# Unread 256-column products at 73 places of a three-layer transformer kernel's TensorE program

## Chip, cores, metric

One core of a Trainium2 chip runs the whole program in one launch. The metric is the device time of that core in microseconds (us). Lower is better.

## What is computed

The input is `x` of 256 tokens by 1024. Three residual layers follow each other, all in float32: one layer of the first kind, a norm, two layers of the second kind, a norm.

```
first kind:   x += 0.5 * swiglu(rms_norm(x));  x += mixer1(rms_norm(x));  x += 0.5 * swiglu(rms_norm(x))
mixer1:       dilated attention (12 heads) and an RWKV-7 recurrence (16 heads), each gated, summed, @ w_o
second kind:  x += 0.5 * swiglu(rmsnorm(x));   x += mixer2(rmsnorm(x));   x += 0.5 * swiglu(rmsnorm(x))
mixer2:       concat(chunked attention, top-k attention, latent attention) @ w_out
```

The feed-forward part is 1024 to 2816 and back. RWKV-7 keeps a 64x64 state per head and updates it by `S = S diag(w) + (S a) b^T + v k^T`.

## The kernel before

**Tiles.** Tokens lie as two halves of 128. A float32 matrix product is made of three products of rounded parts: each operand is split into a high part (`whi`, `xh`, `yh`) and the rest (`wlo`, `xl`, `yl`), and `mm3` (lines 1418 to 1421) multiplies high by high, high by low and low by high. The small products of attention and of the recurrence are plain float32.

**Weights.** They come in chunks of up to 1 MB into three `raw` buffers by SP's queue. ScalarE writes the high part (`split`, line 1939) and VectorE the low part (`split`, line 2284), in two or four pieces a chunk. A piece stands in those engines' programs between the other work, at the place that the order gives it.

**The order.** The class `Order` writes one list of steps, and every engine runs its share of that list in that order. `do` (line 402) appends a step. Eleven stages follow each other: a feed-forward part (stages 0, 2, 4, 6, 7, 9), mixer1 (stage 1), mixer2 (stages 5 and 8), and norms (stages 3 and 10). In mixer1 the recurrence runs as eight groups of two heads (`group`, steps `r_...`), up to three at a time, woven with dense products by a planner that keeps a clock of estimated times (`PACE`, `woven`). In mixer2 the heads, the top-k index, the latent part and the dense products are generators that take turns.

**PSUM.** There are eight banks in a list of free ones. A step takes the bank at the head, and `give` puts it at the end as soon as the steps that read it are written down. On the chip the first product into a bank waits for the last reader of the tile that was there before (`bank_free`, `freed`).

**Steps that the prediction names.** `r_mean` (line 1771) sums a group's result over its heads. `r_d` and `r_x` (lines 1695, 1702, 1683) are the small products by which a 64x64 triangle is inverted; ahead of each `r_x` GpSimd clears a buffer (line 2886). `turn_merged` (line 1439) transposes mixer1's merged rows, which VectorE writes at line 2489. `proj ... in2 3` is the fourth dense product of mixer2, `latent_up` the one ahead of it. `wout2` and `wo` are the last products of the mixers. `warm` (line 1416) makes 12 and 10 products of a zeroed tile at the very start, which nobody reads.

```
class Slots:
    def take(self, key):
        self.at[key] = self.free.pop(0)
    def give(self, key):
        self.free.append((self.at[key][0], key))
```

Of the kernel before, what the change touches and what calls it, by code (L numbers as in the profile page):

```python
# [10 lines left out]
F32R = mybir.dt.float32r  # L11
# [110 lines left out]
    "proj": (("pe", 0.7),), "proj_out": (("dve", 0.7), ("act", 0.6)),  # L122
}
HOP = 0.25


def const_table():
# [67 lines left out]
class Marks:  # L195


    def __init__(self, nc, ctx):
        self.nc, self.ctx = nc, ctx
        self.sem, self.by, self.n, self.at, self.freer = {}, {}, {}, {}, {}  # L200
        self.real = False
        self.had = {}
# [5 lines left out]
    def begin(self, real):  # L208
        self.real = real
        self.had = {}  # L210
        self.n = dict.fromkeys(self.n, 0)
# [21 lines left out]
    def due(self, eng, *tokens):  # L233

        out = {}
        for t in tokens:
            if not t:
                continue
            name, key = t
            if isinstance(key, int):  # L240
                v = key
            elif self.real:
                v = self.at[name][key]
            else:
                v = self.at[name].get(key, 0)
            if self.had.get((eng, name), 0) < v:
                self.had[eng, name] = v
                out[name] = (self.sem[name], v)
        return list(out.values())


class Dry:
# [44 lines left out]
    def max(self, *a, **k):  # L297
        return self
# [54 lines left out]
class Order:  # L353


    def __init__(self, stages):
        self.stages = stages
        self.chunks = plan(stages)
        self.number = {c[:3]: i for i, c in enumerate(self.chunks)}
        last, self.prev = {}, []  # L360
        for i, c in enumerate(self.chunks):
            self.prev.append(last.get(c[4]))
            last[c[4]] = i
        self.steps = []
        self.bank = Slots(range(8))
        self.slots = {}
        self.n_dma = self.n_split = 0
        self.used = set()
        self.lead_from, self.last_from = (), ()
        self.under_way = []  # L370
        self.now, self.ready = {"pe": 0.0, "act": 0.0, "dve": 0.0}, 0.0
        self.begin()
        for s, st in enumerate(stages):
            if st[0] == "ffn":
                self.ffn(s, st[1])
            elif st[0] == "mix1":
                self.mix1(s)
            elif st[0] == "mix2":
                self.mix2(s, st[1])

    def begin(self):

        self.do("warm", 12)
        for _ in range(3):
            self.feed_dma()
        parts = itertools.chain(self.pieces(4), self.pieces(4))
        for nn in range(2):
            self.do("sumsq", 0, 0, nn)
        self.do("scale", 0, 0)
        for k in (0, 2, 4, 6):  # L390
            self.turn(("x", 0, 0, k), "turn_x", 0, 0, k)
            for _ in range({0: 2, 2: 1, 4: 2, 6: 3}[k]):
                next(parts)
            if k == 4:
                for nn in range(2):
                    self.do("sumsq", 0, 1, nn)
        self.do("warm", 10)
        self.do("scale", 0, 1)
        for _ in parts:
            pass  # L400

    def do(self, *step):
        self.steps.append(step)
        for eng, us in PACE.get(step[0], ()):
            self.now[eng] = max(self.now[eng], self.ready) + us
            self.ready = self.now[eng] + HOP

# [691 lines left out]
def build(nc, stages, x_in, wall, consts, rows, lorap, ebias, out):  # L1099
# [5 lines left out]
    with ExitStack() as ctx:  # L1105
        M = Marks(nc, ctx)
# [5 lines left out]
        def sb(name, shape, dt=F32):  # L1112
            return ctx.enter_context(nc.sbuf_tensor(name, shape, dt))
# [5 lines left out]
        xh, xl = sb("xh", [128, 8, 256], F32R), sb("xl", [128, 8, 256], F32R)  # L1119
        yh, yl = sb("yh", [128, 8, 256], F32R), sb("yl", [128, 8, 256], F32R)  # L1120
        C = sb("C", [128, cbase])
        small = sb("small", [128, 84])

        early = [None] * 6
# [9 lines left out]
        PS = ctx.enter_context(nc.psum_tensor("PS", [128, 8, 512], F32))  # L1134

        def con(name):
            a, w = ctab[name]
            return C[:, a:a + w]

# [226 lines left out]
        def run(eng, table):  # L1366
            for name, *a in P.steps:
                if name == "mark":
                    if eng != "sp":
                        M.mark(eng, ("mark",) + tuple(a))  # L1370
                elif name in table:
                    table[name](*a)

        def sync_program(e):
            due = lambda *t: M.due("sp", *t)

            def rows_in(tt):
                e.dma_start(X[:, tt, :], x_in[tt * 128:(tt + 1) * 128]).then_inc(*M.sig(f"x{tt}", ("x",)))

            def load(i):  # L1380
                w = P.chunks[i][3]
                src = wall[int(offs[i]):int(offs[i + 1])].rearrange("(p w) -> p w", p=128)
                if i == 0:
                    rows_in(0)
                    e.dma_start(C[:, 0:chead], consts[:, 0:chead]).then_inc(*M.sig("ident", ("c",)))
                elif i == 1:
                    rows_in(1)
                elif i == 2:
                    e.dma_start(C[:, chead:cbase], consts[:, chead:cbase]).then_inc(*M.sig("consts", ("c",)))
                if i >= 3:  # L1390
# [16 lines left out]
        def tensor_program(e):  # L1407
            due = lambda *t: M.due("pe", *t)
# [9 lines left out]
            def mm3(o, wa, wb, xa, xb, first, last):  # L1418
                e.matmul(o, wa, xa, start=first, stop=False)  # L1419
                e.matmul(o, wa, xb, start=False, stop=False)  # L1420
                return e.matmul(o, wb, xa, start=False, stop=last)  # L1421

            def turned(tile, w, src, *toks):

                b = bank(tile)
                for t in due(bank_free(tile), IDENT, *toks):
                    e.wait_ge(*t)
                for tt in range(2):
                    i = e.transpose(b[0:w, tt * 128:(tt + 1) * 128], src(tt), ident)
                i.then_inc(*M.sig("pe", (tile,)))  # L1430
# [27 lines left out]
            def gu(s, m, i):  # L1458
                hi, lo = whi[slot_of(i)], wlo[slot_of(i)]
                b = bank(("gu", s, m))  # L1460
                for t in due(bank_free(("gu", s, m))):
                    e.wait_ge(*t)
                for g in range(2):
                    for t in due(half_of(i, g == 0)):
                        e.wait_ge(*t)
                    for k in range(8):
                        c0 = (g * 8 + k) * 128
                        for t in due(*[("dve", ("xl", s, tt, k)) for tt in range(2)]):
                            e.wait_ge(*t)
                        p = mm3(b[:, g * 256:(g + 1) * 256], hi[:, c0:c0 + 128], lo[:, c0:c0 + 128], xh[:, k, :],  # L1470
                                xl[:, k, :], k == 0, k == 7)
                p.then_inc(*M.sig("pe", ("gu", s, m), ("use", i)))
# [438 lines left out]
            def turn_out(s, k):  # L1911
                turn_pair(("ot", s, k), OUT, 8, k, *[("dve", ("o", s, kind, tt)) for kind in ("bc" if k >= 4 else "ab")
                                                    for tt in range(2)])

            run("pe", {"warm": warm, "turn_x": turn_x, "gh_turn": gh_turn, "gu": gu, "down": down, "up": up, "wout": wout, "wo": wo, "wout2": wout2,
                       "proj": proj, "shift_mm": shift_mm, "att_qk": att_qk, "att_score": att_score,
                       "att_turn": att_turn, "att_out": att_out, "turn_ao": turn_ao, "turn_merged": turn_merged,
                       "r_lora": r_lora, "r_norm": r_norm, "r_wide": r_wide, "r_vb": r_vb, "r_ka": r_ka,
# [8 lines left out]
        def scalar_program(e):  # L1927
            due = lambda *t: M.due("act", *t)
            COLS = ("ident", ("c",))
            copy = ACT.Copy  # L1930

            def split(i, q, n, after):
                if q < n:
                    w = P.chunks[i][3]
                    c = slice(w * q // n, w * (q + 1) // n)
                    for t in due((f"raw{i % 3}", ("chunk", i)), P.prev[i] is not None and ("pe", ("use", P.prev[i])),
                                 *(marked(*after) if after else ())):
                        e.wait_ge(*t)
                    e.activation(whi[slot_of(i)][:, c].bitcast(F32R), raw[i % 3][:, c], copy).then_inc(  # L1939
                        *M.sig("whi", ("split", i, q)))  # L1940
# [316 lines left out]
            def turn_out(s, k):  # L2257
                high(xh, k, 8, ("ot", s, k), ("oh", s, k))

            run("act", {"out": out_, "split": split, "sumsq": sumsq, "scale": scale, "turn_x": turn_x, "glu": glu,  # L2260
                        "proj_out": proj_out, "shift_copy": shift_copy, "lora_act": lora_act, "att_qk": att_qk,
                        "att_soft": att_soft, "att_turn": att_turn, "turn_ao": turn_ao, "turn_merged": turn_merged,
                        "r_tanh": r_tanh, "r_exp": r_exp, "r_vb": r_vb, "r_ka": r_ka, "r_dm0": r_dm0,
# [531 lines left out]
        def gpsimd_program(e):  # L2795
# [129 lines left out]
            def gain(s):  # L2925
                row = stages[s][1]
                for t in due(*marked("norm", s - 1)):
# [6 lines left out]
                         "r_var": r_var, "bias8": bias8, "m2_begin": m2_begin, "lat_sq": lat_sq, "gain": gain})  # L2934

        programs = (tensor_program, scalar_program, vector_program, gpsimd_program, sync_program)
        M.begin(False)
        for program in programs:
# [9 lines left out]
        @block.tensor  # L2948
        def _(e):
            tensor_program(e)  # L2950

        @block.scalar
        def _(e):
            scalar_program(e)
# [120 lines left out]
```

## Time and profile before

| | |
|---|---|
| median of 3 runs | 1986.04 us (1985.81 to 1987.86) |
| profiled execution, its own time | 1986.59 us |
| its span, first to last instruction | 1984.8 us |
| TensorE products busy | 1903.7 us, 14176 records |
| VectorE, ScalarE, GpSimd busy | 1116.5, 939.5, 91.2 us |
| mean granted TensorE clock | 0.972 |

A record of a product reaches from its start to its modelled end; products follow each other before the one ahead has ended, so the distance of two starts is what one costs. A float32 product that is not a transposition has two records. The row of the granted clock (PEclk) is in tenths of 2.4 GHz, and 0.50 in a stretch means 1.2 GHz throughout. "Idle before" is the time between the modelled end and the next start.

### The profile page before, as it was taken

What the parts mean: (1) busy time and instruction counts of PE and PEld (TensorE: products, weight loads), DVE (VectorE), ACT (ScalarE), POOL (GpSimd) and SP (SyncE); (2) the same over time, 40 slices, a digit from 0 to 9 for tenths busy, and PEclk for the clock granted to TensorE, in tenths of its full rate; (3) what the DMA queues carried; (4) which work ended last, traced back from release to release, by engine and by line L of the source; (5) the groups of instructions that cost most, each with busy time, mean ns of one, the idle gap of its engine ahead of it and who ended that gap; (6) DMA issues with size and microseconds to landing.
All of it is one profiled execution on the core that took longest, in us unless ns stands there. A gap on an engine that the chain in (4) does not pass through costs nothing.

```text
span 1984.8 us, 33483 instructions
## 1 busy us (share of the span) xinstructions
PE 1903.7 (96%) x14176; PEld 1690.7 (85%) x14176; DVE 1116.5 (56%) x2247; ACT 939.5 (47%) x1827; POOL 91.2 (5%) x187
## 2 busy tenths in 40 slices
PE   9999999999998999999999899999999998989998
PEld 8999878888776799979997686899899987868998
DVE  5565556756444555665555745556455657445554
ACT  5454555423211544544554565445444545655443
POOL 0000001111200000010000000000000000000000
PEclk9999999999878999999999999999999999999999
DMA  6564532221101455625562333456355623333553
GB/s 231 188 233 181 186 134 107 94 84 61 55 27 70 157 178 206 233 86 191 210 229 84 107 115 109 170 186 243 123 172 200 241 94 107 107 144 139 191 181 116
DMA packets 42725, 296.28 MB, mean 149 GB/s; under 512 B 4832, under 2 KB 4960, under 8 KB 10576
## 3 DMA queue, kind: packets, MB, share of 16 engines
q1 hardware_dynamic: 41184, 288.32, 40.8%
q0 software_dynamic: 1392, 5.83, 0.9%
q8 instruction: 111, 1.82, 0.4%
q14 instruction: 38, 0.31, 0.0%
HBM read 293.08 MB, written 1.05 MB: 148 GB/s over the span
## 4 chain that ended last, share of the span: by engine, by line
PE 86%; DVE 8%; ACT 3%; POOL 1%; issue 1%; DMA 1%; POOLq 0%; DVEq 0%; ACTq 0%
PE PS L1419 25%; PE PS L1420 23%; PE PS L1421 23%; DVE wlo L2284 1%; PE PS L1702 1%; PE PS L1683 1%; PE PS L1695 1%; DVE xl L2347 1%; ACT GATE L1950 1%; DVE arena L2424 1%; PE PS L1907 1%; PE PS L1819 1%; PE PS L1599 1%; DVE X L2380 1%; PE PS L1447 1%
## 5 line engine op out<-in xcount | busy, mean ns | idle before, releaser
L2284 DVE TENSOR_TENSOR wlo<-raw,whi 128x512 fp32r<-128x512 f32 (+4 forms) x780 | 616.9, 833 | 211.9 <-ACT whi L1939 206.1
L1939 ACT ACTIVATE whi<-raw 128x512 fp32r<-128x512 f32 (+4 forms) x780 | 534.7, 739 | 148.5 <-PE PS L1421 144.7
L1419 PE MATMUL PS<-xh,whi 128*128 128x256 f32 x1944 | 556.0, 286 | 2.1 <-DVE wlo L2284 2.1
L1421 PE MATMUL PS<-xh,wlo 128*128 128x256 f32 x1944 | 550.8, 283 | 0.0
L1420 PE MATMUL PS<-xl,whi 128*128 128x256 f32 x1944 | 550.7, 283 | 0.0
L1419 PEld LDWEIGHTS PS<-xh,whi 128*128 128x128 f32 x1944 | 373.2, 192 | 8.0 <-issue 2.5
L1420 PEld LDWEIGHTS PS<-xl,whi 128*128 128x128 f32 x1944 | 373.2, 192 | 2.3
L1421 PEld LDWEIGHTS PS<-xh,wlo 128*128 128x128 f32 x1944 | 373.1, 192 | 0.0
L1419 PE MATMUL PS<-whi,yh 128*128 128x512 f32 (+2 forms) x580 | 231.3, 399 | 6.9 <-DVE wlo L2284 5.2
L1420 PE MATMUL PS<-wlo,yh 128*128 128x512 f32 (+2 forms) x580 | 227.9, 393 | 0.0
L1421 PE MATMUL PS<-whi,yl 128*128 128x512 f32 (+2 forms) x580 | 227.0, 391 | 0.0
L1419 PE MATMUL PS<-whi,xh 128*128 128x512 f32 (+4 forms) x480 | 196.2, 409 | 13.6 <-DVE wlo L2284 9.6
L2003 ACT ACTIVATE arena<-PS 128x256 f32<-128x256 f32 x108 | 41.4, 383 | 343.8 <-PE PS L1421 343.8
L1420 PE MATMUL PS<-wlo,xh 128*128 128x512 f32 (+4 forms) x480 | 182.7, 381 | 0.0
L1421 PE MATMUL PS<-whi,xl 128*128 128x512 f32 (+4 forms) x480 | 182.3, 380 | 0.0
L2368 DVE TENSOR_TENSOR arena<-arena,PS 128x256 f32<-128x256 f32 x108 | 45.5, 421 | 231.7 <-ACT arena L2003 231.7
L1419 PEld LDWEIGHTS PS<-whi,yh 128*128 128x128 f32 x580 | 111.3, 192 | 30.5 <-DVE wlo L2284 7.8
L1421 PEld LDWEIGHTS PS<-whi,yl 128*128 128x128 f32 x580 | 111.0, 191 | 23.1
L1420 PEld LDWEIGHTS PS<-wlo,yh 128*128 128x128 f32 x580 | 111.3, 192 | 19.3
L1419 PEld LDWEIGHTS PS<-whi,xh 128*128 128x128 f32 x480 | 92.0, 192 | 40.7 <-issue 13.6
L1421 PEld LDWEIGHTS PS<-whi,xl 128*128 128x128 f32 x480 | 92.2, 192 | 14.9
L1420 PEld LDWEIGHTS PS<-wlo,xh 128*128 128x128 f32 x480 | 92.5, 193 | 11.9
(259 smaller groups left out, 2138.7 us busy)
## 6 DMA issues: line engine op xcount, KB each, us to landing
raw<-wall SPq DMA_DIRECT2D x249, 1024.0 KB, 4.9
raw<-wall SPq DMA_DIRECT2D x12, 768.0 KB, 4.2
raw<-wall SPq DMA_DIRECT2D x8, 968.0 KB, 4.9
raw<-wall SPq DMA_DIRECT2D x4, 896.0 KB, 4.4
arena<-ebias POOLq DMA_DIRECT2D x2, 768.0 KB, 4.8
raw<-wall SPq DMA_DIRECT2D x2, 720.0 KB, 4.1
raw<-wall SPq DMA_DIRECT2D x2, 640.0 KB, 3.9
X<-x SPq DMA_DIRECT2D x2, 512.0 KB, 5.1
```

Source lines behind the costliest of these rows:

```text
L1419: e.matmul(o, wa, xa, start=first, stop=False)
L1420: e.matmul(o, wa, xb, start=False, stop=False)
L1421: return e.matmul(o, wb, xa, start=False, stop=last)
L1447: i = e.transpose(b[:, k * 128:(k + 1) * 128], xn[:, tt, (k0 + k) * 128:(k0 + k + 1) * 128], ident)
L1599: p = e.transpose(b[:, c0 + tt * 128:c0 + tt * 128 + 128], src[:, tt * 128:tt * 128 + 128], ident)
L1683: p = e.matmul(b[ps, u * 32:(u + 1) * 32], W_.T[ps, hh, 0, tt, 0:64], some(W_.Dm[ps, u, :], k, 0), start=True, stop=True)
L1695: p = e.matmul(b[ps, u * 32:(u + 1) * 32], W_.DT[ps, u, :], some(X[ps, u, :], k, 0), start=True, stop=True)
L1702: p = e.matmul(b[ps, u * 32:(u + 1) * 32], X[ps, u, :], some(W_.DT[ps, u, :], k, 1), start=True, stop=True)
L1939: e.activation(whi[slot_of(i)][:, c].bitcast(F32R), raw[i % 3][:, c], copy).then_inc(*M.sig("whi", ("split", i, q)))
L2003: e.activation(g, b[:, 0:256], ACT.Silu).then_inc(*M.sig("act", ("silu", s, m)))
L2284: e.tensor_tensor(wlo[slot_of(i)][:, c], raw[i % 3][:, c], whi[slot_of(i)][:, c].bitcast(F32), ALU.subtract).then_inc(*M.sig("wlo", *[("ha ...
L2368: e.tensor_tensor(g, g, b[:, 256:512], ALU.mult).then_inc(*M.sig("dve", ("h", s, m), ("free", ("gu", s, m))))
```

## The change

A table names 73 steps, each with a number. When `do` comes to such a step, it first writes down a step `fill` with that number and with the bank that is at the head of the free list at this moment, which stays in the list. On TensorE `fill` waits for the last reader of that bank's tile and then makes so many products of 128x128 by 128x256 from one tile `still`, all into that bank. Nobody reads them, and the next tile in the bank overwrites them. `still` is a rounded copy of the first 256 columns of the constants (the identity and some that follow it), which ScalarE writes once near the start. The numbers add up to 677: 267 before 38 steps of mixer1 (25 of them steps of the recurrence), 26 before the first product of stage 4 (the middle border), and 192 before 17 steps of each mixer2. All other instructions keep their order.

```diff
+BLANKS = {
+    ('turn_x', 1, 0, 0): 6, ('turn_x', 1, 1, 0): 8, ('proj', 1, 'qkv', 1, 0): 5, ('proj', 1, 'gate', 0, 0): 14,
...
+}
@@ class Order
-        self.steps = []
+        self.steps, self.blanks = [], dict(BLANKS)
...
         self.do("scale", 0, 1)
+        self.do("still")
...
     def do(self, *step):
+        if step[:5] in self.blanks and self.bank.free:
+            self.steps.append(("fill", self.blanks.pop(step[:5])) + self.bank.free[0])
         self.steps.append(step)
@@ build
+        still = sb("still", [128, 256], F32R)
@@ tensor_program
+            def fill(n, i, before):
+                for t in due(M.freed(before), ("act", ("still",))):
+                    e.wait_ge(*t)
+                for _ in range(n):
+                    e.matmul(PS[:, i, 0:256], still[:, 0:128], still[:, :], start=True, stop=True)
@@ scalar_program
+            def still_():
+                for t in due(("consts", ("c",))):
+                    e.wait_ge(*t)
+                e.activation(still[:, :], C[:, 0:256], copy).then_inc(*M.sig("act", ("still",)))
```

TensorE's program at `r_mean` of group 1, before (`L1764` is the last step of the state's chain, `L1771` is `r_mean`, `L1683` an `r_x`):

```order
L1764 MATMUL PS<-arena 64x64 [waits dve]
L1764 MATMUL PS<-arena 64x64
L1771 MATMUL PS<-arena,C 128x256 [waits act,dve]
L1683 MATMUL PS<-arena 64x32 [waits dve]
L1683 MATMUL PS<-arena 64x32 x7
```

and with the change (lines are 27 or 34 higher there; `L1455` is `fill`):

```order
L1798 MATMUL PS<-arena 64x64 [waits dve]
L1798 MATMUL PS<-arena 64x64
L1455 MATMUL PS<-still 128x256 [waits dve]
L1455 MATMUL PS<-still 128x256 x18
L1805 MATMUL PS<-arena,C 128x256 [waits act]
L1717 MATMUL PS<-arena 64x32 [waits dve]
L1717 MATMUL PS<-arena 64x32 x7
```

The wait for VectorE, which is for the bank, moved from `r_mean` to the first of 19 unread products; the wait for ScalarE stayed.

TensorE's program with the change where mixer2's last `latent_up` (128x320) ends and `proj in2 3` (128x512) begins:

```order
L1448 MATMUL PS<-whi,yl 128x320
L1455 MATMUL PS<-still 128x256 [waits act]
L1455 MATMUL PS<-still 128x256 x37
L1446 MATMUL PS<-whi,xh 128x512 [waits wlo]
L1447 MATMUL PS<-wlo,xh 128x512
```

Before, the 128x512 product stood right behind the 128x320 one and waited for ScalarE and for the low half of its weights; now 38 products stand between, the first of which waits for ScalarE.

## Rows read from the trace of the kernel before

**Rows 1.** The page: the granted clock in 40 slices of 49.6 us.
```profile
PEclk9999999999878999999999999999999999999999
```

**Rows 2.** The view of the cores: span and mean granted clock.
```profile
core 0: 1984.8 us, clock 0.972
```

**Rows 3.** Busy time by stretch, mixer1 and behind: length, PE, PEld, DVE, ACT, POOL, clock.
```profile
348.99:352.40 3.41, 3.41 (x16) 3.23 (x16) 3.37 (x7) 0.70 (x2) 0.00 (x0) 0.50 0.31 72
...
441.15:451.39 10.24, 9.01 (x95) 7.47 (x91) 4.20 (x14) 1.11 (x3) 1.27 (x2) 0.50 0.01 2
...
526.48:540.13 13.65, 12.94 (x146) 11.19 (x144) 2.58 (x11) 1.46 (x4) 1.57 (x3) 0.50 0.01 1
546.96:553.79 6.83, 6.83 (x64) 5.57 (x61) 1.58 (x6) 2.19 (x6) 0.00 (x0) 0.50 0.01 2
564.02:581.09 17.07, 16.36 (x140) 13.03 (x140) 7.04 (x20) 4.19 (x11) 1.62 (x3) 0.50 0.01 1
615.23:622.06 6.83, 6.38 (x52) 5.37 (x54) 1.83 (x7) 0.13 (x1) 1.03 (x1) 0.50 0.00 0
628.88:635.71 6.83, 5.87 (x17) 4.08 (x17) 2.27 (x6) 0.60 (x2) 1.04 (x1) 0.50 0.00 0
642.53:649.36 6.83, 5.90 (x22) 5.42 (x23) 5.24 (x12) 3.20 (x10) 0.00 (x0) 0.50 0.08 32
867.81:871.22 3.41, 3.41 (x11) 2.73 (x10) 0.67 (x3) 0.36 (x2) 1.52 (x3) 0.50 0.01 2
```

**Rows 4.** The same view: the stretches at 1.2 GHz in the first mixer2.
```profile
1113.57:1116.98 3.41, 3.41 (x15) 3.41 (x14) 3.31 (x11) 2.52 (x6) 0.00 (x0) 0.50 0.46 193
1120.40:1123.81 3.41, 3.41 (x9) 2.64 (x10) 3.34 (x13) 0.00 (x0) 0.00 (x0) 0.50 0.16 29
1215.97:1222.80 6.83, 6.05 (x19) 4.62 (x17) 5.49 (x8) 5.10 (x8) 0.00 (x0) 0.50 0.52 188
```

**Rows 5.** The same view: 4 us ahead of a fall, and 3.41 us ahead of a rise.
```profile
437.15:441.15 4.00, 1.84 (x19) 1.14 (x19) 2.64 (x8) 0.75 (x3) 0.00 (x0) 1.00 0.00 0
...
7.65:11.06 3.41, 3.41 (x18) 3.41 (x17) 2.14 (x6) 3.14 (x10) 0.00 (x0) 0.50 1.01 419
```

**Rows 6.** Timeline of TensorE at the start: start, duration, engine, line, operation.
```profile
8.95 3.41 PE L1416 MATMUL PS<-arena 128*128 128x128 f32 x20
```

**Rows 7.** Timeline of TensorE: the second and the 27th start of products in a row.
```profile
215.62 0.28 PE L1420 MATMUL PS<-xl,whi 128*128 128x256 f32 x1
...
218.62 0.28 PE L1421 MATMUL PS<-xh,wlo 128*128 128x256 f32 x1
```

**Rows 8.** Timeline of TensorE, `wout2` in stage 5: four starts.
```profile
1222.33 0.62 PE L1420 MATMUL PS<-wlo,xh 128*128 128x512 f32 x1
1222.76 0.42 PE L1421 MATMUL PS<-whi,xl 128*128 128x512 f32 x1
1223.02 0.40 PE L1419 MATMUL PS<-whi,xh 128*128 128x512 f32 x1
1223.25 0.39 PE L1420 MATMUL PS<-wlo,xh 128*128 128x512 f32 x1
```

**Rows 9.** Timeline of TensorE at four of the 73 places; idle before, releaser in brackets.
```profile
279.44 0.55 PE L1558 MATMUL PS<-C,arena 128*128 128x128 f32 x3 [0.55 <-ACT arena L2065]
...
440.30 0.67 PE L1771 MATMUL PS<-arena,C 128*128 128x256 f32 x2 [2.16 <-DVE yl L2673]
...
643.46 1.33 PE L1439 MATMUL PS<-C,GATE 128*128 128x128 f32 x5 [3.12 <-DVE GATE L2489]
...
1120.29 0.72 PE L1419 MATMUL PS<-whi,xh 128*128 128x512 f32 x1 [2.90 <-DVE wlo L2284]
```

**Rows 10.** Timeline of VectorE ahead of `r_mean` of group 1.
```profile
438.96 0.42 DVE L2669 TENSOR_TENSOR arena<-arena,PS 128x256 f32<-128x256 f32 x1
```

**Rows 11.** Timeline of TensorE at two waits of the recurrence that get no products.
```profile
524.70 0.48 PE L1695 MATMUL PS<-arena 64*64 64x32 f32 x10 [1.19 <-DVE arena L2600]
...
545.39 0.42 PE L1695 MATMUL PS<-arena 64*64 64x32 f32 x8 [1.60 <-DVE arena L2600]
```

More of the change, by code:

```diff
@@ L124 @@
 HOP = 0.25
+BLANKS = {
+    ('turn_x', 1, 0, 0): 6, ('turn_x', 1, 1, 0): 8, ('proj', 1, 'qkv', 1, 0): 5, ('proj', 1, 'gate', 0, 0): 14,
+    ('proj', 1, 'gate', 0, 4): 2, ('att_turn', 1, 0, 0, 0): 13, ('turn_ao', 1): 3, ('up', 1, 0, 0, 0): 12,
+    ('shift_mm', 1, ('v', 1), 0, 0): 17, ('r_s', 1, 1, 2): 4, ('r_mean', 1, 1): 19, ('r_d', 1, 2, 4): 10,
+    ('r_x', 1, 2, 5): 3, ('r_d', 1, 2, 5): 4, ('r_rp', 1, 2): 3, ('r_s', 1, 2, 3): 11, ('r_lora', 1, 6): 3,
+    ('r_g0', 1, 5): 3, ('r_d', 1, 4, 5): 5, ('r_d', 1, 5, 3): 4, ('r_yp', 1, 4): 2, ('r_s', 1, 5, 2): 10,
+    ('r_s', 1, 5, 3): 4, ('r_x', 1, 6, 2): 5, ('r_d', 1, 6, 3): 7, ('r_x', 1, 7, 5): 5, ('r_d', 1, 7, 5): 3,
+    ('r_rp', 1, 7): 7, ('r_s', 1, 7, 1): 2, ('r_s', 1, 7, 2): 3, ('r_s', 1, 7, 3): 3, ('r_mean', 1, 7): 5,
+    ('r_var', 1, 7): 8, ('r_turn2', 1, 7): 6, ('turn_merged', 1, 0): 35, ('wo', 1, 1, 0, 0): 6,
+    ('wo', 1, 2, 0, 0): 5, ('wo', 1, 2, 1, 0): 2, ('proj', 4, 'gh', 0, 0): 26, ('turn_x', 5, 0, 0): 6,
+    ('turn_x', 5, 1, 0): 9, ('turn_iq', 5): 19, ('proj', 5, 'in2', 2, 4): 9, ('lat_turn', 5, 0, 0): 13,
+    ('latent_up', 5, 'ukv', 0, 0): 18, ('proj', 5, 'in2', 3, 0): 38, ('turn_c', 5, 0): 4,
+    ('u_turn', 5, 'c', 0, 0): 4, ('turn_b', 5, 0): 11, ('u_out', 5, 'a', 0, 0): 7, ('wout2', 5, 2, 0, 0): 10,
+    ('u_out', 5, 'a', 4, 1): 14, ('turn_out', 5, 2): 8, ('wout2', 5, 1, 0, 0): 9, ('wout2', 5, 0, 0, 0): 11,
+    ('wout2', 5, 0, 1, 0): 2, ('turn_x', 8, 0, 0): 6, ('turn_x', 8, 1, 0): 9, ('turn_iq', 8): 19,
+    ('proj', 8, 'in2', 2, 4): 9, ('lat_turn', 8, 0, 0): 13, ('latent_up', 8, 'ukv', 0, 0): 18,
+    ('proj', 8, 'in2', 3, 0): 38, ('turn_c', 8, 0): 4, ('u_turn', 8, 'c', 0, 0): 4, ('turn_b', 8, 0): 11,
+    ('u_out', 8, 'a', 0, 0): 7, ('wout2', 8, 2, 0, 0): 10, ('u_out', 8, 'a', 4, 1): 14, ('turn_out', 8, 2): 8,
+    ('wout2', 8, 1, 0, 0): 9, ('wout2', 8, 0, 0, 0): 11, ('wout2', 8, 0, 1, 0): 2,
+}
 def const_table():
@@ L1913, in turn_out @@
                                                     for tt in range(2)])
-            run("pe", {"warm": warm, "turn_x": turn_x, "gh_turn": gh_turn, "gu": gu, "down": down, "up": up, "wout": wout, "wo": wo, "wout2": wout2,
+            run("pe", {"fill": fill, "warm": warm, "turn_x": turn_x, "gh_turn": gh_turn, "gu": gu, "down": down, "up": up, "wout": wout, "wo": wo, "wout2": wout2,
                        "proj": proj, "shift_mm": shift_mm, "att_qk": att_qk, "att_score": att_score,
@@ L2258, in turn_out @@
                 high(xh, k, 8, ("ot", s, k), ("oh", s, k))
-            run("act", {"out": out_, "split": split, "sumsq": sumsq, "scale": scale, "turn_x": turn_x, "glu": glu,
+            run("act", {"still": still_, "out": out_, "split": split, "sumsq": sumsq, "scale": scale, "turn_x": turn_x, "glu": glu,
                         "proj_out": proj_out, "shift_copy": shift_copy, "lora_act": lora_act, "att_qk": att_qk,
```

## The prediction

> **What bounds the kernel now.** TensorE has work nearly everywhere, so the questions are at which clock it runs and where it waits. I read the granted clock first, then busy time by stretch, then single waits in the timeline. The mean clock is 0.972 over 1984.8 us [rows 2], so 0.028 of the span, 55.6 us, is the most that the clock can have cost; the slices show that most of it lies in one part, the second half of mixer1 [rows 1]. There are two levels only: cutting the time at the places where the level changes gives stretches with 0.50, that is 1.2 GHz, throughout, and 1.00 between them. Ahead of a fall TensorE did little: of the 4 us before the fall at 441.15 its products fill 1.84 us [rows 5], since `r_mean` stood idle for 2.16 us [rows 9].
>
> The stretches at 1.2 GHz that lie behind the first products of the change are nine from mixer1 to stage 4 [rows 3] and three in the first mixer2 [rows 4], which the second mixer2 repeats with the same lengths. At 1.2 GHz a 512-column product costs 0.43 us (1222.33 to 1222.76), at 2.4 GHz 0.23 us (1223.02 to 1223.25) [rows 8]. So half of the busy time of such a stretch is what the clock costs in it.
>
> **The change: what it gives.** If no fall is left behind the first products, TensorE gets back half of its busy time in these stretches:
> - the recurrence, six stretches from 441.15 to 635.71: 9.01 + 12.94 + 6.83 + 16.36 + 6.38 + 5.87 = 57.4 us, half is 28.7;
> - 348.99, 642.53 and 867.81: 3.41 + 5.90 + 3.41 = 12.7, half is 6.4;
> - mixer2: 3.41 + 3.41 + 6.05 = 12.9, half is 6.4, twice 12.9.
>
> Together 48.0 us. That unread products count for the clock is shown at the start of the same trace: most of the stretch from 7.65 to 11.06, after which the clock rose [rows 5], is filled by `warm`, 20 records of products of a zeroed tile from 8.95 on [rows 6].
>
> **What it costs.** A 256-column product of rounded operands with its own load of weights costs 0.12 us at 2.4 GHz: from the second start to the 27th are 25 steps in 3.00 us [rows 7]. All 677 are 81.2 us. They are in the engine's order ahead of the step that waits, so they are free up to the length of the wait. The wait that a product can use is 0.16 us longer than the idle time shown, as a record lasts 0.28 us and the next may start after 0.12 us. Place by place:
> - `proj in2 3`: 38 x 0.12 = 4.56 us against 2.90 + 0.16 = 3.06 us [rows 9]: 1.5 us over, in both mixer2, 3.0.
> - `wout2` of the last chunk gets 11 and 2 products, 1.56 us, at a step (1223.02) that comes 0.26 us behind the one before and waits for nothing [rows 8]: 3.1 in both.
> - `turn_merged`: 35 x 0.12 = 4.20 against 3.12 + 0.16 [rows 9]: 0.9.
> - `r_mean` of group 1: its first unread product waits for VectorE, as the order shows. The tile's reader ends at 439.38 [rows 10]; 19 x 0.12 = 2.28 us from there ends 1.4 us behind 440.30, when the step starts today.
> - The softmax transposition at 279.44: 13 x 0.12 = 1.56 against 0.55 + 0.16 [rows 9]: 0.85.
> - The same comparison at the other places finds 30 more where the products are longer than the wait, by 0.7 us at most and 7.4 us together, and 34 where they are not.
>
> That is 16.7 us. It is the same loss in two guises. Where the numbers exceed today's wait, either the products are simply late, or the wait has grown by then because TensorE comes sooner to something that another engine times. The second is plain at `proj in2 3`: VectorE is busy for 3.31 of 3.41 us in the stretch at 1113.57 [rows 4] and the wait is for VectorE's low half, so the 1.7 us that the clock gives back there is waited away at 1120.29. I take the whole 16.7 us. Its bounds are 0 (all waits stay, and all late products find a wait behind them) and about 27 us: 16.7 and another 10, if the gained time beside VectorE's and ScalarE's work of mixer2 (12.9 us, of which 3.0 + 3.1 are in the sum already) and of the border (3.0) is waited away too.
>
> **What stays slow.** Two waits of the recurrence get no products: 1.19 us before 524.70 and 1.60 us before 545.39 [rows 11]. Each stands right ahead of a fall, those at 526.48 and 546.96, whose stretches hold (12.94 + 6.83) / 2 = 9.9 us of the gain [rows 3]. Earlier steps come sooner, so these waits may move away or stay. I take half, 4.9 us lost; the ends are 0 and 9.9.
>
> **The new ScalarE step.** `still` is one copy of 256 columns near 16 us, ahead of a piece of a weight split. No row shows just it; bounds are 0, and 0.5 us, if TensorE waits for the whole of it. I take 0.4. The other instructions, the DMAs and their queues keep their order. The feed-forward parts are untouched and start when their predecessor ends.
>
> **Sum.** 48.0 - 16.7 - 4.9 - 0.4 = 26.0 us less. Against the profiled execution's own time of 1986.59 us that is 1960.6; this one was 0.55 us above the median of the runs shown, so the forecast is **1960 us**.
>
> Here the Trainium skill speaks against one term. The page TensorE: Matmul & The Clock Gate, part 4 on the PE-mode transpose, says that transpositions do not count as busy for the gate in the way products do. The stretch at 642.53 holds the 16 transpositions of `turn_merged`; by that rule it would stay slow, and the sum would be 3.0 us smaller, 1963. The unread products ahead of it are ordinary ones, which is why I count it in.
>
> **Rivals.**
>
> *A. The recurrence does not hold the clock.* Its small products use 64 rows and 32 columns, and six of the stretches lie in it, one after another, two behind waits without products. If it falls back each time and only the clean cases outside are won, the gain is 48.0 - 28.7 = 19.3, less 16.7 and 0.4: 1984. For it: the two unfilled waits, and the few products at most of its places (2 to 11, but for 19 at one). Against: between 451.39 and 526.48 the recurrence ran for 75 us without a fall.
>
> *B. All of the gain stays.* The numbers fit waits that are longer in the new program, and late products find a wait behind them. Then 48.0 - 0.4 go: 1938 from the median. Against: VectorE's full time in mixer2 [rows 4].
>
> *C. Slower.* One mechanism: the products stand ahead of the awaited step and run to their end. If the clock falls as often as today, because products of constants that sit behind a bank's wait come too late to keep it, nothing is won and every excess is a delay: 1986 + 16.7 + 0.4 = 2003. It decides the sign where less than 17.1 of the 48.0 us comes back. Products at 1.2 GHz would cost more still.
>
> *D. By the page's rule.* The clock is worth little, wherever it falls: in the recurrence the time goes from TensorE to VectorE and back whatever the clock, and only the stretches of dense products outside it have something to give, 6.4 + 12.9 = 19.3 us. Less 17.1 that is about 1984, as in A, but with the clock back at 1.00 throughout. The Trainium skill (TensorE: Matmul & The Clock Gate, part 1) says that for modeling the ramp penalty is under 1% of a typical span; 1% here is an estimate of 19.8 us. The trace disagrees: half of the busy time in these stretches is 48.0 us, 2.4%.
>
> *E. Nothing happens,* since gain and excess cancel or the products do not count: 1986.
>
> **Numbers.** Forecast 0.64, B 0.13, A 0.08, D 0.03, C 0.06, E 0.06. The forecast's own range is 1960 with the bounds of its terms: 4.9 more back and 7 of the 16.7 found as waits gives 1948; the other half of the two stretches and 8 us more waited away gives 1973. The cases besides hold 0.36; with most of B's side and what lies between the forecast and A taken in, the range is 1943 to 1979. What a measurement of this kernel can tell from no change is 0.2%, 4 us. A and D lie 2 us under the median and so within it, though half of their chance is for a partial gain that can be told. Faster: 0.64 + 0.13 + 0.06 = 0.83. Within: 0.05 + 0.06 = 0.11. Slower: C, 0.06.
>
> **What would show it.** The mean clock should rise from 0.972 to 0.985 or more, and the stretches at 441, 564, 628, 642, 867, 1113, 1216 should read 1.00. If the forecast's doubt is right, a fall remains near the two unfilled waits. PE's busy time between 437 and 440 should start only after VectorE's reader. `proj in2 3` should start about as late as today, measured from the start of its stage. It is wrong if the recurrence (from 349 to 640) shrinks by less than 10 us, if the clock is back and the time is not, or if mixer2 gains over 5 us each.

## Result, and the profile after

The changed kernel takes 1973.98 us, median of 4 runs (1970.99 to 1977.1); the kernel before takes 1985.92 us in 4 runs beside it (1983.79 to 1987.86). The ratio is 0.9948, with a 95% interval of [0.9928, 0.9969]: faster, by 12 us, where 26 were forecast. The profiled execution is the fastest of the four, 1970.99 us.

The page after: busy time of each engine, the granted clock in 40 slices, and the shares of the chain that ended last.
```profile
PE 1944.0 (99%) x14853; PEld 1743.4 (89%) x14853; DVE 1115.8 (57%) x2247; ACT 939.1 (48%) x1828; POOL 90.8 (5%) x187
...
PEclk9999999999899999999999999999999999999999
...
PE 93%; DVE 4%; ACT 2%; POOL 1%; DMA 1%; issue 0%; SPq 0%; POOLq 0%; DVEq 0%; ACTq 0%
```
The view of the cores after.
```profile
core 0: 1969.2 us, clock 0.997
```
TensorE has 677 more records and the other engines' work is unchanged. The clock stands at 0.997 where it was 0.972 [rows 2]; only one of 40 slices is below 9, where three read 8, 7 and 8 [rows 1].

Busy time by stretch after: all before the one slow stretch, that stretch, and all behind it; the 4 us up to the moment at which the recurrence first fell before (compare [rows 5]); a stretch with mixer1's transpositions; and the 15 us of mixer2 that end with `proj in2 3`. Columns as in [rows 3].
```profile
0.00:526.98 526.98, 518.20 (x4906) 462.56 (x4907) 308.11 (x664) 244.87 (x499) 49.08 (x81) 1.00 0.41 146
526.98:537.22 10.24, 10.24 (x109) 9.16 (x105) 1.86 (x8) 1.43 (x4) 1.56 (x3) 0.50 0.01 2
537.22:1969.20 1431.98, 1415.51 (x9847) 1271.70 (x9846) 805.80 (x1575) 692.81 (x1326) 40.15 (x103) 1.00 0.43 153
437.17:441.17 4.00, 2.71 (x21) 2.25 (x21) 2.34 (x7) 0.75 (x3) 0.00 (x0) 1.00 0.00 0
630.00:637.00 7.00, 6.80 (x45) 5.89 (x44) 5.91 (x14) 3.72 (x11) 0.00 (x0) 1.00 0.14 59
1091.30:1106.50 15.20, 15.11 (x103) 14.25 (x101) 13.09 (x44) 7.75 (x17) 0.00 (x0) 1.00 0.30 112
```
All stretches at 1.2 GHz of [rows 3, 4] are gone, the short one of the start [rows 5] too. One is left, of 10.24 us, besides the last microseconds, in which TensorE has nothing to do. So the clock came back and half of the expected time did not.

**Where the time went.** All products of the kernel before also stand in the changed one, in the same order. I took the distance from each start to the next in both traces, with the two records of a plain float32 product taken as one, and sorted the differences by what happened there. This sum is over some 12,400 distances and no row of a view shows it; rows for its main parts follow.

| distances between old products (us, after less before) | all | recurrence | border of mixer1 | each mixer2 |
|---|---|---|---|---|
| at 1.2 GHz before, at 2.4 GHz after | -38.2 | -19.7 | -2.3 | -5.7 |
| those that hold one of the 73 places | +20.9 | +6.7 | +2.1 | +5.3 |
| at 2.4 GHz in both | +1.7 | | | |
| sum (the spans: 1969.2 less 1984.8) | -15.6 | | | |

The clock gave 38.2 us and the places took 20.9 of them back. The median is 12 us below before and not 15.6; the other three runs of the changed kernel had lower clocks, 0.993 to 0.995. Of the 1.7 us at 2.4 GHz in both, the start holds +2.5 and all that follows -0.8.

Timeline of TensorE after, at five places: `r_mean` of group 1, the one remaining fall, `turn_merged`, `proj in2 3`, `wout2` of the last chunk.
```profile
438.16 0.33 PE L1798 MATMUL PS<-arena 64*64 64x64 f32 x4
439.78 2.53 PE L1455 MATMUL PS<-still 128*128 128x256 f32 x19 [1.29 <-DVE arena L2708]
442.15 0.59 PE L1805 MATMUL PS<-arena,C 128*128 128x256 f32 x2
...
524.69 0.66 PE L1729 MATMUL PS<-arena 64*64 64x32 f32 x16 [1.19 <-DVE arena L2639]
...
536.10 1.22 PE L1455 MATMUL PS<-still 128*128 128x256 f32 x4
537.25 0.66 PE L1729 MATMUL PS<-arena 64*64 64x32 f32 x16
...
627.28 4.35 PE L1455 MATMUL PS<-still 128*128 128x256 f32 x35
631.47 1.03 PE L1473 MATMUL PS<-C,GATE 128*128 128x128 f32 x8
...
1101.83 0.31 PE L1448 MATMUL PS<-whi,yl 128*128 128x320 f32 x1
1101.98 4.71 PE L1455 MATMUL PS<-still 128*128 128x256 f32 x38
1106.57 0.50 PE L1446 MATMUL PS<-whi,xh 128*128 128x512 f32 x1
...
1205.96 1.47 PE L1455 MATMUL PS<-still 128*128 128x256 f32 x11
1207.27 0.49 PE L1446 MATMUL PS<-whi,xh 128*128 128x512 f32 x1
```
- `r_mean`: TensorE still idles 1.29 us, for VectorE's reader of the bank that the unread products use, and 19 of them then hold the step back. It starts 1.9 us later than before [rows 9], in a program that was 0.4 us later already (435.24 before, 435.59 after, at the place ahead): 1.5 us lost.
- The wait without products ahead of 524.69 stayed at 1.19 us, as in [rows 11], and the fall at 526.98 follows it. Four unread products that lie in the slow stretch cost 1.15 us (536.10 to 537.25), twice their price.
- `proj in2 3`: the product now waits from 1101.98 to 1106.57, 4.6 us, where it waited 3.1. The 1.5 us that the clock gives back ahead of it are waited away there. VectorE is as busy as before: 13.09 of 15.20 us above, and 13.07 in the same part of the trace before:
```profile
1105.00:1120.20 15.20, 10.16 (x47) 8.91 (x45) 13.07 (x44) 7.97 (x17) 0.00 (x0) 0.89 0.30 111
```
And VectorE finishes the low half of the weights that the product needs just when the step starts. Timeline of VectorE, after:
```profile
1105.83 0.69 DVE L2323 TENSOR_TENSOR wlo<-raw,whi 128x512 fp32r<-128x512 f32 x1
```
The runs with other numbers settle whose time this is. Timeline of TensorE of `e6_no_mixer2`, which has no product at this place:
```profile
1103.99 0.50 PE L1436 MATMUL PS<-whi,xh 128*128 128x512 f32 x1 [3.01 <-DVE wlo L2313]
```
Measured from `turn_x` at the stage's start (1054.14 before, 1039.54 after), the step starts at 66.1 us with no product there (before, `e6_no_mixer2`, `e8_mixed`), with 19 (`e4_half`) and with 38 (`e1_trim`, `e5_two_waits`, `e9_both`), at either clock. In the kernels with the change's own numbers in mixer2 (the change, `e2_mixer2`, `e7_zeros`, `e10_change_again`) it starts at 67.0, since places ahead of it are late there: already the last `latent_up` ahead of it comes 0.9 us later.
- `wout2`: 11 products, 1.3 us from 1205.96 to 1207.27, at a step that waited for nothing before [rows 8].

The shares of the chain that ended last fit this: TensorE 93% instead of 86%, VectorE 4% instead of 8%. The page's share by line gives 4% to `L1455`, the unread products: they stand where the chain ran through VectorE and ScalarE before.

### The profile page after: what moved, and what is told of

The parts are those of the page before. It is cut to its first block, busy times and chain, and to the rows that moved or that the text cites. A ratio compares the mean times of both kernels' runs of the same rounds, so it can differ in the third digit from the quotient of the medians.

```text
span 1969.2 us, 34831 instructions
## 1 busy us (share of the span) xinstructions
PE 1944.0 (99%) x14853; PEld 1743.4 (89%) x14853; DVE 1115.8 (57%) x2247; ACT 939.1 (48%) x1828; POOL 90.8 (5%) x187
## 4 chain that ended last, share of the span: by engine, by line
PE 93%; DVE 4%; ACT 2%; POOL 1%; DMA 1%; issue 0%; SPq 0%; POOLq 0%; DVEq 0%; ACTq 0%
PE PS L1446 26%; PE PS L1447 25%; PE PS L1448 25%; PE PS L1455 4%; PE PS L1717 1%; PE PS L1736 1%; PE PS L1941 1%; PE PS L1729 1%; PE PS L1481 1%; DMA raw<-wall 1%; PE PS L1853 1%; PE PS L1905 1%; PE PS L1930 1%; PE PS L1633 1%; DVE wlo L2323 1%; PE PS L1897 1%
## 5 line engine op out<-in xcount | busy, mean ns | idle before, releaser
L1447 PEld LDWEIGHTS PS<-wlo,xh 128*128 128x128 f32 x480 | 90.5, 188 | 11.3
```

## Experiments

The **first theory**: the clock's gain is real, and late products at the places eat it; whatever takes products off where they are late brings time. Its **rival**: the gain itself is small, since VectorE or ScalarE time these parts whatever the clock is; then taking products off brings nothing. One run asks besides whether it matters what the products multiply.

No kernel below leaves out or changes any product that is read.

| kernel | unread products, places | median us (range, runs) | ratio to before [95%] | clock of the runs |
|---|---|---|---|---|
| `e1_trim` | 549, 67 | 1967.7 (1960.13 to 1970.55, 6) | 0.991 [0.9893, 0.9927] | 0.990 to 0.997 |
| `e2_mixer2` | 384, 34 | 1982.31 (1978.1 to 1985.87, 12) | 0.999 [0.9978, 1.0002] | 0.980 to 0.986 |
| `e3_two_more` | 823, 73 | 1980.95 (1979.1 to 1987.44, 12) | 0.9985 [0.9975, 0.9995] | 0.993 to 0.998 |
| `e4_half` | 357, 73 | 1969.85 (1967.12 to 1974.5, 6) | 0.9926 [0.9911, 0.9942] | 0.990 to 0.993 |
| `e5_two_waits` | 568, 69 | 1961.72 (1958.06 to 1965.75, 4) | 0.989 [0.987, 0.991] | 0.993 to 0.998 |
| `e6_no_mixer2` | 209, 33 | 1971.88 (1969.43 to 1978.03, 6) | 0.9945 [0.9926, 0.9963] | 0.982 to 0.987 |
| `e7_zeros` | 677, 73 | 1974.85 (1972.07 to 1976.34, 5) | 0.9953 [0.9937, 0.997] | 0.993 to 0.996 |
| `e8_mixed` | 264, 39 | 1963.44 (1962.0 to 1967.44, 4) | 0.9901 [0.9883, 0.992] | 0.989 to 0.994 |
| `e9_both` | 604, 73 | 1958.61 (1958.45 to 1959.96, 4) | 0.9871 [0.9852, 0.9889] | 0.998 to 0.999 |
| `e10_change_again` | 677, 73 | 1971.64 (1969.05 to 1977.48, 6) | 0.9933 [0.9915, 0.9951] | 0.992 to 0.997 |

Before had medians of 1985.05 us beside the first four, 1984.06 beside `e5` to `e8`, 1986.23 beside the last two. "Places" and "clock's gain" below are the first two lines of the sum above, taken of the profiled execution of each.

### e1_trim: only as many products as the wait holds

At each place I took off as many as made the awaited step late in the changed kernel's trace.
```diff
-    ('r_mean', 1, 1): 19, ('r_d', 1, 2, 4): 10, ('r_lora', 1, 6): 3, ('r_d', 1, 6, 3): 7,
+    ('r_mean', 1, 1): 5, ('r_d', 1, 2, 4): 2,
...
-    ('lat_turn', 5, 0, 0): 13, ('turn_iq', 5): 19,
+    ('lat_turn', 5, 0, 0): 6, ('turn_iq', 5): 16,
```


> The change with its numbers cut by what each place was late in its own profile: 549 products at 67 places instead of 677 at 73; r_mean of group 1 keeps 5 of 19, att_turn and lat_turn 6 of 13, six places none. Theory 1 (lateness): in the changed kernel the steps behind the products start 18.3 us in sum after what they wait for is ready, of which 0.04 us at each of 73 places is the hop that was there before; the other 15.4 us are on the path. Then this kernel is 10 to 15 us faster than the change, 1960 to 1964 us, 1.1 to 1.3% under the kernel before, with the clock still at 0.99. Theory 2 (hidden gain): the excess over the old waits is a wait that another engine times; taking products away gives idle time in their place and the time stays at 1971 to 1974. Theory 3 (the clock needs all of them): fewer products in the recurrence let the clock fall again, below 0.985, and the time is 1975 or more.

Six us faster than the change by the medians, from other sets of runs; its intervals and `e10_change_again`'s overlap, and the median misses the expected 1960 to 1964 by 4 us. The comparison at equal clock is sharper: 1966.82 us at 0.992 and 1964.79 at 0.993 stand against the change's 1977.48 and 1977.1, some 11 us. In its fastest, profiled, execution it is 10.9 us faster (span 1958.3 against 1969.2, both at 0.997). The clock's gain there is 37.2 us, as before the trim (38.2); the places fell from 20.9 to 9.4. So of the change's 20.9 us, 11.5 were products too many. Of the 9.4 left, 7.6 lie in the two mixer2, where the wait is real. Timeline of TensorE of `e1_trim` there:
```profile
1092.48 4.71 PE L1454 MATMUL PS<-still 128*128 128x256 f32 x38
1097.07 0.49 PE L1445 MATMUL PS<-whi,xh 128*128 128x512 f32 x1
```
The same 4.6 us as in the change: nothing is late, another engine sets this time. The first theory holds, and the rival for this one place. But the spread of this kernel's runs, 10 us, goes with its clock: 1960.13 us at 0.997, 1964.79 at 0.993, 1970.55 at 0.990. With fewer products the recurrence falls in some executions and not in others.

### e2_mixer2: mixer2's products alone

```diff
-    ('turn_x', 1, 0, 0): 6, ... ('proj', 4, 'gh', 0, 0): 26,
     ('turn_x', 5, 0, 0): 6, ...
```


> Only the products of the two mixer2 (34 places, 384 products); none in mixer1 and at the middle border. From the two traces, the change starts stage 6 only 0.55 us earlier against stage 5's start than before, and 0.45 in the second mixer2, although all three falls of the clock in each are gone. Hidden gain: the kernel is 1 us faster than before, 1985. If the three stretches at 1.2 GHz were worth what half of their busy time says, 6.4 us each, less the 2.9 us of lateness, it would be 7 us faster, 1979. The clock should come back from 0.972 to about 0.985 in both.

The ratio, 0.999 [0.9978, 1.0002], can't be told from no change. Each mixer2 gets 5.7 us from the clock and gives 5.3 at the places. All slow stretches in its two parts are gone, as two stretches of its profile show (from 700 us on the clock is 1.00, and mixer1, which has no products, keeps its falls):
```profile
0.00:700.00 700.00, 666.39 (x6406) 580.10 (x6407) 396.10 (x878) 298.53 (x615) 64.31 (x110) 0.95 0.36 129
700.00:1980.40 1280.40, 1266.29 (x8156) 1146.81 (x8155) 719.46 (x1370) 641.22 (x1213) 27.19 (x77) 1.00 0.46 161
```
The medians are 2.7 us apart, with the expected 1 us between. So 34 places and 384 products bring next to nothing.

### e3_two_more: two more products at every place

```diff
-    ('turn_x', 1, 0, 0): 6, ('turn_x', 1, 1, 0): 8, ...
+    ('turn_x', 1, 0, 0): 8, ('turn_x', 1, 1, 0): 10, ...
```


> Two products more at each of the 73 places: 146 more, 17.5 us at 0.12 us. Lateness: nearly every place already ends at or after the moment when its step is ready, so all of it is on the path: 15 to 18 us slower than the change, 1988 to 1992. Hidden gain: if waits behind the places take up what is late, clearly less, 5 to 10 us slower than the change, 1979 to 1984.

146 more products are 17.5 us at 0.12. The places rose from 20.9 to 34.3, so 13.4 of them came through: most waits were full. The median is 7.0 us above the change's, 9.3 above `e10_change_again`'s. So the 15 to 18 us of the first theory missed, and 1980.95 us lies where the rival had put it (1979 to 1984). Two things stand between: 4.1 us did find a wait, and the clock was higher in most runs (0.996 to 0.998). At equal clock it is 1987.44 us against 1977.1 at 0.993 and 1981.8 or 1980.63 against 1970.99 at 0.997, some 10 us.

### e4_half: half of the products, rounded up

```diff
-    ('r_mean', 1, 1): 19, ('proj', 5, 'in2', 3, 0): 38, ...
+    ('r_mean', 1, 1): 10, ('proj', 5, 'in2', 3, 0): 19, ...
```


> Half of the products at every place (357). Lateness is gone at nearly all of them, so only the clock tells. If a part of a wait filled with products is enough to hold the clock, it stays at 0.99 and the time is as in the trimmed kernel, 1960 to 1964. If the wait must be nearly filled, the clock falls at the long waits again, the mean is 0.98, and the time is 1970 to 1978.

By the medians faster than the change by 4 us, or by 1.8 against `e10_change_again`, which the intervals can't tell from nothing, and at a lower clock: 0.990 to 0.993. That lies between the two expected ranges. In its profile the clock's gain is 30.3 us and the places take 12.3. Half of the products hold most of the clock.

### e5_two_waits: the two unfilled waits get products

The trimmed numbers, and 10 and 9 products ahead of the fourth `r_d` of groups 4 and 5. The last reader of the bank at the head of the free list is there the step that `r_d` waits for itself; so these go into the bank that `r_d` itself is about to write.
```diff
+OWN = (('r_d', 1, 4, 4), ('r_d', 1, 5, 4))
...
+            own = self.bank.at[("Dd",) + step[2:4]] if step[:5] in OWN else self.bank.free[0]
-            self.steps.append(("fill", self.blanks.pop(step[:5])) + self.bank.free[0])
+            self.steps.append(("fill", self.blanks.pop(step[:5])) + own)
```


> The trimmed kernel (e1_trim) and products at the two waits of the recurrence that had none, 10 before r_d of group 4 and 9 before r_d of group 5, made in the bank that r_d itself is about to write, so that they wait for nothing. In the trimmed kernel's profile 3.4 us at 1.2 GHz are left behind the first of them, and in the change's 10.2 us. If the fall there comes from this wait, it is gone, and the runs that have clock 0.990 to 0.993 with the trimmed numbers come up to 0.994 or more: the median goes from 1967.7 to 1962 to 1965. If the clock there is decided by the small products of the recurrence and not by the wait, the clock and the time stay as in e1_trim.

Timeline of TensorE of `e5_two_waits` at the first of the two:
```profile
519.94 0.30 PE L1801 MATMUL PS<-arena 64*64 64x64 f32 x4
520.17 1.46 PE L1458 MATMUL PS<-still 128*128 128x256 f32 x10
521.56 0.66 PE L1732 MATMUL PS<-arena 64*64 64x32 f32 x16
```
The wait is filled, and no fall follows it. This is hardly chance: all seven profiles (one execution of each kernel) of the changed kernel and of experiments in which this wait is unfilled and the recurrence has products (`e1`, `e3`, `e4`, `e6`, `e7`, `e10`) have a fall between 521.8 and 528.0, and none of the three in which it is filled (`e5`, `e8`, `e9`). Two others remain in `e5_two_waits`, at 444.12 (3.41 us) and 597.72 (6.83 us). The median is 6 us below `e1_trim`'s, but from another set of runs, and the intervals of the two ratios overlap (0.9893 to 0.991). `e5_two_waits` fills a second wait too, but that one lies behind the fall and can't be its cause. So it is shown, as far as ten profiles can, that this wait decides that fall; that it costs some 5 us agrees with the medians, and is less sure.

### e6_no_mixer2: the trimmed numbers, none in mixer2

```diff
-    ('turn_x', 5, 0, 0): 5, ... ('wout2', 8, 0, 1, 0): 2,
```


> The trimmed kernel without any product in the two mixer2: 33 places of mixer1 and the middle border are left. With the products there, the three stretches at 1.2 GHz of each mixer2 give back 5.7 us and the same places grow by 3.8 us in the trimmed kernel. So 1.9 us are at stake in each mixer2: 2 to 4 us slower than e1_trim, 1970 to 1972, with the clock lower by 0.007 to 0.010. If the 5.7 us were all worth time, it would be 11 us slower, 1979; if nothing is, it is as fast as e1_trim.

0.9945, as good as the whole change with less than a third of its products, and 1971.88 us is what was expected. `e1_trim` has 0.991, and the two intervals barely touch, so trimmed products in mixer2 are not worthless.

### e7_zeros: the same products of a tile of zeros

```diff
-                e.activation(still[:, :], C[:, 0:256], copy).then_inc(*M.sig("act", ("still",)))
+                e.activation(still[:, :], C[:, 0:256], copy, scale=0.0).then_inc(*M.sig("act", ("still",)))
```


> The change with a tile of zeros in place of the constants, same 677 products. If the clock is granted for products whatever they multiply, as the start's warm products of zeros suggest, clock 0.993 to 0.997 and 1971 to 1977 as for the change. If values matter, the clock stays near 0.975 and all products are cost: 1990 or more.

1974.85 us against 1973.98 and 1971.64: no difference that can be told. Zeros do as well as this tile. But the operand of 128x128 is the identity in the change too, so most of what it multiplies by is zero already; dense values on both sides were not tried.

### e8_mixed and e9_both: more where the clock is fragile, fewer elsewhere

`e8_mixed` has nearly the change's numbers in the recurrence (fewer or none at the five places with over 0.8 us of late products), the trimmed ones elsewhere in mixer1 and in stage 4, both waits filled, and none in mixer2. `e9_both` adds the trimmed mixer2.
```diff
     ('r_s', 1, 1, 2): 4, ('r_mean', 1, 1): 7, ('r_d', 1, 2, 4): 5, ('r_d', 1, 5, 3): 2, ('r_d', 1, 6, 3): 3,
+    ('r_d', 1, 4, 4): 10, ('r_d', 1, 5, 4): 9,
+    ('turn_x', 5, 0, 0): 5, ('turn_iq', 5): 16, ('proj', 5, 'in2', 3, 0): 38, ...
```
(the last line is `e9_both`'s alone)

> 264 products at 39 places: in the recurrence nearly the numbers of the change (r_mean of group 1 with 7 of 19, r_lora without, three r_d with half), the trimmed numbers at the other places of mixer1 and the border, the two waits of e5_two_waits with products, none in mixer2. Fewer falls than in e1_trim in the recurrence should outweigh up to 3 us more of lateness there: in the recurrence it is as fast as e1_trim or up to 3 us faster, and it lacks the 2 to 4 us of mixer2: 1966 to 1971. If lateness outweighs, 1972 to 1975.

> e8_mixed with the trimmed products of the two mixer2 added: 604 products at 73 places. e8_mixed left the six stretches at 1.2 GHz in mixer2 and had 1963.4; adding the products there is worth 2 to 5 us each way of reckoning (1.9 us a mixer by the places, 10 us in sum between e1_trim and e6_no_mixer2 less what mixer1 did differently): 1958 to 1961, clock 0.997, the fastest of all. If lateness in the recurrence is what limits, it is no faster than e5_two_waits, 1962.

`e8_mixed` came out 2.6 us under its range. In its profile, in the recurrence the clock's gain is 22.5 us and the places take 2.3. Its other runs reach down to a clock of 0.989, so they may fall elsewhere too. Mixer2 keeps its slow stretches; by stretch, of `e8_mixed`:
```profile
1095.32:1098.73 3.41, 3.32 (x8) 2.64 (x9) 3.34 (x12) 0.00 (x0) 0.00 (x0) 0.50 0.11 20
1190.90:1197.73 6.83, 6.05 (x19) 4.71 (x18) 5.08 (x8) 5.10 (x8) 0.00 (x0) 0.50 0.52 197
```
`e9_both` is the fastest of all, 0.9871 [0.9852, 0.9889], 27.6 us under before, and the only one whose runs agree within 1.5 us. By stretch, its first 11.25 us and all the rest:
```profile
0.00:11.25 11.25, 8.22 (x43) 8.06 (x44) 3.57 (x10) 5.95 (x14) 1.20 (x7) 0.85 0.85 324
11.25:1956.70 1945.45, 1926.34 (x14739) 1725.08 (x14738) 1112.11 (x2238) 933.05 (x1815) 90.17 (x180) 1.00 0.42 150
```
The clock stays up from 11.25 us to the last product. In mixer2 it gains 5.7 us and pays 3.8 at the places: 1.9 us in each, where the full numbers leave 0.5.

### e10_change_again: the change as it is

No edit. 

> The change itself once more, beside e9_both on the same chip: 1971 to 1977 with clock 0.993 to 0.997 as before, 12 us under the kernel before and 12 to 16 us over e9_both. If its 12 us was an accident of its four runs, it comes out elsewhere, for example at 1960 as was forecast.

The ratio is 0.9933 [0.9915, 0.9951]; with the first result there are ten runs between 1969.05 and 1977.48. Its slowest, profiled, fell at the same place as the change's first profile and stayed down twice as long, 20.48 us, and fell once more at 607.78 for 10.24 us. Timeline and stretch of `e10_change_again`:
```profile
523.81 0.66 PE L1729 MATMUL PS<-arena 64*64 64x32 f32 x16 [1.19 <-DVE arena L2639]
```
```profile
525.86:546.34 20.48, 20.48 (x242) 18.22 (x242) 6.28 (x22) 2.08 (x6) 1.57 (x3) 0.50 0.01 2
```
The unfilled wait is the same 1.19 us to the hundredth, and what follows it differs.

## Why the prediction was right in sign and wrong in size

Columns of the table are us taken from the time, a cost negative. The direction and the mechanism held, and the time lies in the stated range (1943 to 1979); the gain was 12 us where 26 were forecast, less than half. For the profiled executions 26.0 stand against 15.6. Term by term:

| term | forecast | measured |
|---|---|---|
| clock, recurrence | 28.7 - 4.9 = 23.8 | 19.7 |
| clock, 348.99, 642.53, 867.81 | 6.4 | 5.4 |
| clock, both mixer2 | 12.8 | 11.4 |
| places named in the text | -9.3 | -9.6 |
| the other places | -7.4 | -11.3 |
| `still` | -0.4 | 0.0 |
| the start, ahead of `still` | 0 | -0.8 |
| other, at 2.4 GHz in both | 0 | +0.8 |
| sum | 26.0 | 15.6 |

(The clock's 1.7 us at the start, where the stretch of [rows 5] is gone, stand in the start's row: TensorE waited 1.7 us more at 12.19 for VectorE, and by 15.5 us was 0.8 us later than before. `still` runs only at 16.67 and moves TensorE's products by no more than 0.05 us. The same program again, `e10_change_again`, is 0.05 us later there and not 0.8. So the term for `still` was too high, and that the start cost about as much is luck.)

**The failed step is the sum's two large terms, both mis-sized in the same direction, by 6.6 and 4.2 us.**

*"So half of the busy time of such a stretch is what the clock costs in it."* It is less, for two reasons. The profiles of `e8_mixed` and `e9_both`, which have no fall in the recurrence, get 22.5 us back there and not 28.7. First, of the recurrence's 57.4 us of busy time 50.8 lie between old products with no place between them. The other 6.6 lie ahead of a place, in part as the last product there up to its modelled end: when it runs faster, the wait behind it begins sooner, and what of that reaches the end is part of the places' sum. Half of 6.6 is 3.3 us. Second, the 50.8 us give back 22.5, or 0.44 of them, and not half, which is 2.9 us: a product at 2.4 GHz costs more than half of one at 1.2. The rows said so for 512 columns, 0.23 us against 0.43 [rows 8]. Inside the recurrence's runs of 64x32 products 16.4 us became 9.1 in `e9_both`, and where one step hands over to the next that waits for another engine less still comes back. Outside the recurrence the second reason does most of it (16.8 of 19.2): the stretches at 348.99 and 867.81 hold no place between their products and gave 1.6 us each of 3.41.

*"The same comparison at the other places finds 30 more ... 7.4 us together."* The five kinds of place that I looked at one by one came out at 9.6 us against 9.3: `in2 3` 3.1 (3.0), `wout2` 3.3 (3.1), `turn_merged` 0.9 (0.9), `r_mean` 1.5 (1.4), the softmax transposition 0.8 (0.85). The rest, compared with the waits of before, came out at 11.3. That comparison took waits from a program that no longer exists: the gap is not the same once TensorE comes to it sooner. Most of the cost was products that are late by the new trace, as `e1_trim` shows, whose cut by that trace brings 11.5 us in its profile and some 11 at equal clock. One place cost more since its products lay at 1.2 GHz (536.10: 1.3 us more than before). The upper bound of 27 us held.

*"I take half, 4.9 us lost."* Right in size here: one stretch of 10.24 us stayed, half is 5.1, behind one of the two waits, and `e5_two_waits` speaks for that cause. That the size fits is luck: in `e10_change_again`, the same program, 20.48 us stayed behind that wait and 10.24 more further on.

*The median.* The forecast treated the clock as a property of the kernel. It is one of an execution: the changed kernel's runs range from 0.992 to 0.997 and 8.4 us. The profiled execution was the best of its four; their median lies 3.0 us above it. Before, 1977.08 to 1986.94 us in one set, at 0.981 and 0.973, shows that the spread was there already.

**The rivals.** A (the recurrence does not hold): no; it gave half of the gain. B (all stays): no; 9.4 us remain at the places even in the trimmed kernel. C (slower): its price of 17.1 us was too low if anything, 21, but the gain of 38 stood against it. D: the Trainium skill (TensorE: Matmul & The Clock Gate, part 1) puts the ramp penalty below 1% of a typical span. It says so where it speaks of the slow products at a kernel's start, and D, and the prediction's "the trace disagrees", took it for falls in mid-kernel as well. These cost more here: 38.2 us came from the clock, 1.9% of the span, and `e9_both` keeps 1.3% of the time. Its part 4, that transpositions do not count as busy in the way products do, would have left the stretch of `turn_merged` slow; the stretch 630.00:637.00 above holds them and reads 1.00. No run here tells whether they count by themselves, since 35 products stand ahead of them.

**What it said would show.** Clock at 0.985 or more, the named stretches at 1.00, the fall near an unfilled wait, unread products only after VectorE's reader, `in2 3` as late as before, measured from the stage's start: at 66.2 us (1120.29 less 1054.14) before and 67.0 after (1106.57 less 1039.54). All came; `in2 3` was 0.9 us later, for places ahead of it that were late. From 348.37 to 643.46 before are 295.1 us, after (350.23 to 631.47) 281.2: 13.9 less, above the 10 that would have made it wrong.

## What to carry to other kernels

Time on the clock and time at the end are two sums: before pricing a slow stretch, take off the products that stand right ahead of a wait on another engine, price the rest by rows at both clocks and not by half, and in a part that VectorE times expect next to nothing. Unread products that hold TensorE's clock are free only up to the wait that the *new* program has, so give them by a trace of the changed program and cut them once: here the cut alone made 12 us into 17, and with two more waits filled and the recurrence fuller it was 27. Where the clock falls in some executions only, a change's worth is that of many runs, and waits filled to the end look like the safer choice in the fragile part: the four runs of `e9_both` are the only ones that agree so closely.

## What the hardware showed beside

- The clock fell behind a wait as short as 1.19 us when only small products stood around it (64 rows, 32 columns), and not once between 11.25 us and the last product of `e9_both`'s profile, though TensorE was still idle for 1.3 us at `r_mean`. A longer wait among small products, 1.44 us before 544.74 in the change's trace, had no fall behind it. So the length of one wait does not decide.
- Products of zeros held it as well as those whose one operand is the identity: 0.993 to 0.996 against 0.992 to 0.997.
- The same program, with the same 1.19 us of wait, stayed at 1.2 GHz for 10.24 us in one execution and 20.48 us in another. What decides this no run here shows.
- A slow stretch that is left makes the cure dearer: the 4 unread products inside one cost 0.29 us each, against 0.12 outside.
